# A new order of the query chunks in a differential attention stage

## The chip, the cores and the metric

The kernel runs on one core of one Trainium2 chip. The metric is the device time of one execution in microseconds (us), as the median of three runs. The engines are named as in the profile: PE is TensorE (matmul), PEld its weight load, DVE is VectorE, ACT is ScalarE, POOL is GpSimd, SP is SyncE, which issues the DMAs. Each engine works through its own instructions strictly in the order in which the program lists them; engines wait for one another through semaphores.

## The reference

Two transformer blocks are computed one after the other for 1024 tokens of width 1024. The change touches one stage of the second block, the differential attention of four heads. For each head there are two score maps, their softmaxes are subtracted with a factor, and the difference weighs the values:

```python
def diff_group(dq, dk, dv, q_g, k_g, lq1, lk1, lq2, lk2, out_g, rel_bias, lam_init):
    q = rms_norm(dq.reshape(b, s, DIFF_HEADS, 2, DIFF_QK), q_g)
    k = rms_norm(dk.reshape(b, s, DIFF_HEADS, 2, DIFF_QK), k_g)
    ...
    def one_block(args):
        qb, blk = args                       # 128 query tokens
        allowed = chunk_allowed(q_idx, k_idx)  # 64-token chunks up to the query's own
        bias = table[t5_bucket(k_idx[None, :] - q_idx[:, None])].transpose(2, 0, 1)
        logits = jnp.einsum('bhqmd,bhmkd->bhmqk', qb, k_t).astype(f32) * scale
        logits = logits + bias[None, :, None]
        logits = jnp.where(allowed[None, None, None], logits, NEG_INF)
        probs = jax.nn.softmax(logits, axis=-1)
        attn = (probs[:, :, 0] - lam * probs[:, :, 1]).astype(v_t.dtype)
        return jnp.einsum('bhqk,bhkd->bhqd', attn, v_t)
```

Query chunk t (0 to 7) sees the key tiles 0 to t only. The eight chunks of a head are independent of one another, so they can be computed in any order.

## The kernel before

The program is written out by hand, engine by engine, with one function for each stage and engine. The differential attention is `pe_diff`, `act_diff` and `dve_diff`, with `pe_diff_values`, `act_diff_copies`, `diff_turn` and the preparation of the next head (`pe_diff_prepare`, `act_diff_norms`, `act_diff_parts`, `dve_diff_norms`, `dve_diff_parts`) beside them.

The work is cut into 32 items, one for each head and query chunk. Item n belongs to head n // 8, and `diff_item(n)` says which chunk t it takes. Its size S is t + 1 key tiles of 128 tokens. Before the change the sizes run 1, 2, ..., 8 in heads 0 and 2 and 8, 7, ..., 1 in heads 1 and 3. All engines run the same loop over steps; in step s

- PE first makes four transposes of the next head's queries or keys (L2501), but only in steps 4 to 7 of a head that has a successor. Then it makes the scores of item s (L2638, and the mask L2641). Then it transposes the weights of item s-3 in blocks of up to four tiles (L2651) into PSUM bank 6, and behind each such block it multiplies the block before by the values (L2671). An item of five to eight tiles has two blocks; it is called a two-block item here. For it, the values of its first block stand in its own step, behind its second block's transposes.
- ACT first makes, in steps 4 to 7, the high part of the next head's queries or keys out of bank 6 (L2531). Then come the copy of item s-3's first block (L2694), the exponentials of item s in two passes (L2723), with the copy of a second block between them, and at the end of some steps a square (L2510, L2514) or a root for the next head's norms.
- DVE first makes the low part (L2562) in steps 4 to 7. Then come the weights of item s-2 (L2771, L2773, L2778), the two bias passes of item s (L2790), which read the scores out of PSUM, and the "put" of item s-4 (L2797), which moves the finished output out of bank 7. At the end of some steps it adds a reduction (L2539) or a product (L2548) for the next head: reductions at the end of step 7 and of step 0, products at the end of steps 2 and 3.

The waits that matter are these. The scores of item n+1 wait for the first bias pass of item n. The values of item n's first block wait for the put of item n-1, as both use bank 7:

```python
        if c == 0 and n:
            pe.wait_ge(*self.s("df_put").at(n - 1))
```

The next head's transposes and the turned blocks share bank 6, so each waits until ACT and DVE have read what stands there (`turn_bank_free`). Behind the last item, PE puts the first matmuls of the next stage (L2867 to L2869, `pe_mla_up`) between the rest of the items' blocks.

Of the kernel before, what the change touches and what calls it, by code (L numbers as in the profile page):

```python
# [19 lines left out]
TT = T // P  # L20
# [65 lines left out]
class Kernel:  # L86
# [2341 lines left out]
    def score(self, p, cols, qh, ql, kh, kl):  # L2428
# [4 lines left out]
                mm = self.mm3([self.PS[:, 2 * p + h, 0:n]], qh, ql, [kh[:, c]], [kl[:, c]], True, True)  # L2433
        return mm

    def diff_item(self, n):
        h, t = n // TT, n % TT
        return h, t if h % 2 == 0 else TT - 1 - t

    def groups(self, ap, c=64):  # L2440
        return ap.rearrange("p (g c) -> p g c", c=c)
# [1046 lines left out]
```

## Time and profile before

| | us |
|---|---|
| median of three runs | 2967.72 |
| lowest and highest | 2965.39, 2972.66 |
| the profiled execution | 2988.82 |
| its span, first to last instruction | 2987.5 |
| PE busy in the span | 2875.9 (96%) |
| DVE busy | 1858.2 (62%) |
| ACT busy | 1204.7 (40%) |
| granted TensorE clock, mean over the span | 0.967 |

The profiled execution is 21.1 us longer than the median of the runs. PE is busy nearly all the time, but not everywhere: the second line of the page, which cuts the span into 40 slices, shows 7 and 7 tenths in the slices from 1718 to 1867 us. This is the differential attention. In those slices the granted clock is also below full speed.

### The profile page before, as it was taken

The page shows a single profiled execution, that of the slowest core. Times are in us where ns is not written, and L with a number is a line of the kernel's source. Part 1 is how long each engine was busy: PE and PEld are TensorE (multiplying, and loading weights), DVE is VectorE, ACT ScalarE, POOL GpSimd, SP SyncE. Part 2 cuts the span into 40 slices and gives each one's busy share as a digit, 9 for nine tenths or more (in the row PEclk, how much of TensorE's full clock was granted, in tenths as well). Part 3 has the DMA queues.
Part 4 walks back from the last instruction along what each step waited for, and adds up shares of the span by engine and source line. Part 5 has one row for each costly group of instructions (what it writes and reads, how often), then busy time and mean ns, then how long its engine had stood idle before and what let it go on. Part 6 is the DMA issues. An engine that isn't in the chain of part 4 may idle for free.

```text
span 2987.5 us, 36065 instructions
## 1 busy us (share of the span) xinstructions
PE 2875.9 (96%) x14312; PEld 2407.0 (81%) x14312; DVE 1858.2 (62%) x2615; ACT 1204.7 (40%) x1810; POOL 68.9 (2%) x44
## 2 busy tenths in 40 slices
PE   8999999999999999999999977899999999999998
PEld 6888878887788888888778856788887888888887
DVE  4148766625766666666641277577457777777774
ACT  3144454634433323334331265776433333333432
POOL 0002210010000000000000000000000000000000
PEclk9999997999999999999999988888999999999999
DMA  4111220032211111113121100000211111111122
GB/s 169 50 36 57 79 99 1 6 123 78 106 56 50 51 57 52 50 54 127 50 92 57 37 14 10 22 1 1 92 43 42 50 57 57 47 53 57 56 93 85
DMA packets 47831, 172.99 MB, mean 58 GB/s; under 512 B 5648, under 2 KB 6160, under 8 KB 47664
## 3 DMA queue, kind: packets, MB, share of 16 engines
q1 hardware_dynamic: 47664, 170.68, 17.1%
q8 instruction: 115, 1.88, 0.3%
q14 instruction: 52, 0.43, 0.0%
HBM read 145.23 MB, written 25.43 MB: 57 GB/s over the span
## 4 chain that ended last, share of the span: by engine, by line
PE 87%; DVE 8%; ACT 3%; issue 2%; DMA 0%; SPq 0%; DVEq 0%; ACTq 0%
PE PS L295 14%; PE PS L297 14%; PE PS L299 14%; PE PS L1598 8%; PE PS L1599 8%; PE PS L1600 8%; PE PS L483 2%; PE PS L485 2%; PE PS L484 2%; PE PS L1186 2%; PE PS L706 2%; PE PS L1156 1%; PE PS L1171 1%; PE PS L3118 1%; DVE H L2790 1%
## 5 line engine op out<-in xcount | busy, mean ns | idle before, releaser
L289 DVE TENSOR_TENSOR w_lo<-w_raw,w_hi 128x1024 fp32r<-128x1024 f32 x93 | 117.1, 1262 | 203.1 <-ACT w_hi L283 203.1
L1598 PE MATMUL PS<-u_hi_f,w_hi 128*128 128x512 f32 x624 | 242.7, 389 | 0.0
L1599 PE MATMUL PS<-u_lo_f,w_hi 128*128 128x512 f32 x624 | 242.7, 389 | 0.0
L1600 PE MATMUL PS<-u_hi_f,w_lo 128*128 128x512 f32 x624 | 242.7, 389 | 0.0
L1547 ACT ACTIVATE w_hi<-weight_sums 128x512 fp32r<-128x512 f32 x156 | 98.1, 629 | 356.0 <-DVE weight_sums L1568 197.1
L283 ACT ACTIVATE w_hi<-w_raw 128x1024 fp32r<-128x1024 f32 x93 | 97.6, 1054 | 263.4 <-PE PS L485 136.5
L295 PE MATMUL PS<-f_ah,w_hi 128*128 128x512 f32 x640 | 197.1, 389 | 0.1
L297 PE MATMUL PS<-f_al,w_hi 128*128 128x512 f32 x640 | 197.0, 389 | 0.0
L299 PE MATMUL PS<-f_ah,w_lo 128*128 128x512 f32 x640 | 197.0, 389 | 0.0
L1553 DVE TENSOR_TENSOR w_lo<-w_raw,w_hi 128x512 fp32r<-128x512 f32 x205 | 137.3, 688 | 92.9 <-ACT w_hi L1547 92.9
L1598 PE MATMUL PS<-f_T_hi,w_hi 128*128 128x512 f32 x468 | 182.8, 390 | 1.9 <-issue 1.9
L1600 PE MATMUL PS<-f_T_hi,w_lo 128*128 128x512 f32 x468 | 182.8, 391 | 0.0
L1599 PE MATMUL PS<-f_T_lo,w_hi 128*128 128x512 f32 x468 | 182.6, 390 | 0.0
L1553 DVE TENSOR_TENSOR w_lo<-weight_sums,w_hi 128x512 fp32r<-128x512 f32 x156 | 107.2, 687 | 62.2 <-ACT w_hi L1547 62.2
L295 PEld LDWEIGHTS PS<-f_ah,w_hi 128*128 128x128 f32 x640 | 120.1, 188 | 25.3 <-issue 0.5
L297 PEld LDWEIGHTS PS<-f_al,w_hi 128*128 128x128 f32 x640 | 120.1, 188 | 25.0
L299 PEld LDWEIGHTS PS<-f_ah,w_lo 128*128 128x128 f32 x640 | 120.1, 188 | 24.9
L295 PE MATMUL PS<-u_hi,w_hi 128*128 128x512 f32 x384 | 126.9, 412 | 13.5 <-DVE u_lo L416 13.5
L1598 PEld LDWEIGHTS PS<-u_hi_f,w_hi 128*128 128x128 f32 x624 | 117.1, 188 | 24.4
L1599 PEld LDWEIGHTS PS<-u_lo_f,w_hi 128*128 128x128 f32 x624 | 117.1, 188 | 24.3
L1600 PEld LDWEIGHTS PS<-u_hi_f,w_lo 128*128 128x128 f32 x624 | 117.1, 188 | 24.3
L1660 DVE TENSOR_TENSOR Y<-Y,PS 128x1024 f32<-128x1024 f32 x80 | 97.6, 1220 | 52.3 <-PE PS L299 52.3
(447 smaller groups left out, 6612.4 us busy)
## 6 DMA issues: line engine op xcount, KB each, us to landing
w_raw<-in_weights SPq DMA_DIRECT2D x215, 512.0 KB, 3.6
H<-in_x_t SPq DMA_DIRECT2D x16, 512.0 KB, 4.3
h_kept<-H SPq DMA_DIRECT2D x16, 512.0 KB, 5.1
H<-h_kept SPq DMA_DIRECT2D x16, 512.0 KB, 6.7
stick_kept<-stick_stage SPq DMA_DIRECT2D x12, 512.0 KB, 2.8
mixer<-stick_kept SPq DMA_DIRECT2D x9, 512.0 KB, 6.8
p_kept<-p_stage SPq DMA_DIRECT2D x8, 512.0 KB, 4.0
p_pp<-p_kept SPq DMA_DIRECT2D x8, 512.0 KB, 8.1
```

The source lines that it names most:

```text
L283: act.activation(self.w_hi[i][:], self.w_raw[i][:], ACT.Copy).then_inc(*self.s("w_hi").up(g))
L289: dve.tensor_tensor(self.w_lo[i][:], self.w_raw[i][:], self.w_hi[i][:].bitcast(F32), ALU.subtract).then_inc(*self.s("w_lo").up(g))
L295: ins = e.matmul(banks[i], lh, rh[i], start=first, stop=False)
L297: ins = e.matmul(banks[i], lh, rl[i], start=False, stop=False)
L299: ins = e.matmul(banks[i], ll, rh[i], start=False, stop=last)
L483: pe.matmul(self.PS[:, t, :], UH[:, k, tok], wh, start=first, stop=False)
L1547: act.activation(self.w_hi[room][:, cols], src, ACT.Copy).then_inc(*self.s("w_hi").up("block", n, m))
L1553: dve.tensor_tensor(self.w_lo[room][:, cols], src, self.w_hi[room][:, cols].bitcast(F32), ALU.subtract).then_inc(*self.s("w_lo").up("block ...
L1598: pe.matmul(out, hi[:, self.chunk(k)], rh, start=opens and k == 0, stop=False, skip_group_check=True)
L1599: pe.matmul(out, hi[:, self.chunk(k)], rl, start=False, stop=False, skip_group_check=True)
L1600: mm = pe.matmul(out, lo[:, self.chunk(k)], rh, start=False, stop=k == 3, skip_group_check=True)
L1660: dve.tensor_tensor(Y[:, c, :], Y[:, c, :], self.pair(p), ALU.add).then_inc(*self.dve_frees(p, tag, "down", i, c))
```

## The change

Every head now takes its query chunks in the order 2, 5, 4, 3, 1, 7, 6, 0, so that the sizes run 3, 6, 5, 4, 2, 8, 7, 1 in each head.

```diff
+    DIFF_ORDER = (2, 5, 4, 3, 1, 7, 6, 0)
+
     def diff_item(self, n):
-        h, t = n // TT, n % TT
-        return h, t if h % 2 == 0 else TT - 1 - t
+        return n // TT, self.DIFF_ORDER[n % TT]
```

The number and the shapes of the instructions stay the same. They are listed in another order on PE, ACT and DVE. The line numbers of the stage go up by one.

The first place is step 4 of the second head on PE, from the scores to the transposes that open step 5. In a row, df_kh and df_qh are parts of keys and queries, ident with H is a block being turned, df_at with mixer_196 are the turned weights and the values, and df_staged is the next head. Before:

```order
L2638 MATMUL PS<-df_kh_206,df_qh_204 128x512 x2
L2638 MATMUL PS<-df_kl_207,df_qh_204 128x512 x2
L2638 MATMUL PS<-df_kh_206,df_ql_205 128x512 x2
L2641 MATMUL PS<-df_mask,sb_ident 128x128 x2
L2651 MATMUL PS<-ident,H 128x128 x4
L2671 MATMUL PS<-mixer_196,df_at_212 128x128 x4
L2651 MATMUL PS<-ident,H 128x128 x3
L2671 MATMUL PS<-mixer_196,df_at_211 128x128 x4
L2501 MATMUL PS<-ident,df_staged_219 128x128 x4
```

Now:

```order
L2639 MATMUL PS<-df_kh_206,df_qh_204 128x256 x2
L2639 MATMUL PS<-df_kl_207,df_qh_204 128x256 x2
L2639 MATMUL PS<-df_kh_206,df_ql_205 128x256 x2
L2642 MATMUL PS<-df_mask,sb_ident 128x128 x2
L2652 MATMUL PS<-ident,H 128x128 x4
L2672 MATMUL PS<-mixer_196,df_at_211 128x128 x3
L2652 MATMUL PS<-ident,H 128x128 x2
L2672 MATMUL PS<-mixer_196,df_at_212 128x128 x4
L2502 MATMUL PS<-ident,df_staged_219 128x128 x4
```

The scores in this step shrink from four key tiles to two, and the item being turned from seven tiles (four and three) to six (four and two). Both before and now, four values matmuls and then the next head's transposes stand at the end.

The second place is DVE in step 5 of the second head, from the low part (L2562, now L2563) to the first bias pass (ISA). Before:

```order
L2562 SCALAR_TENSOR_TENSOR df_ql_201<-PS,df_gq,df_qh_200 128x512
L2771 RECIPROCAL df_small<-df_small 128x2
L2773 TENSOR_SCALAR df_small<-df_small,df_nlam 128x1
L2778 SCALAR_TENSOR_TENSOR H<-H,df_small 128x640
L2790 ISA H,df_small<-PS,df_bias_209 128x384
```

Now:

```order
L2563 SCALAR_TENSOR_TENSOR df_ql_201<-PS,df_gq,df_qh_200 128x512
L2772 RECIPROCAL df_small<-df_small 128x2
L2774 TENSOR_SCALAR df_small<-df_small,df_nlam 128x1
L2779 SCALAR_TENSOR_TENSOR H<-H,df_small 128x512
L2791 ISA H,df_small<-PS,df_bias_209 128x1024
```

The bias pass at this place grows from three tiles to eight, and the weights product before it shrinks from five tiles to four.

The third place is the end of the stage on PE, from the last item's mask to the first matmul of the next stage. Before:

```order
L2641 MATMUL PS<-df_mask,sb_ident 128x128 x2
L2651 MATMUL PS<-ident,H 128x128 x4
L2671 MATMUL PS<-mixer_196,df_at_212 128x128
L2651 MATMUL PS<-ident,H 128x128 x3
L2671 MATMUL PS<-mixer_196,df_at_211 128x128 x4
L2867 MATMUL PS<-w_hi_53,mla_lh_223 128x384
```

Now:

```order
L2642 MATMUL PS<-df_mask,sb_ident 128x128 x2
L2652 MATMUL PS<-ident,H 128x128 x2
L2672 MATMUL PS<-mixer_196,df_at_212 128x128 x4
L2652 MATMUL PS<-ident,H 128x128 x4
L2672 MATMUL PS<-mixer_196,df_at_211 128x128 x2
L2652 MATMUL PS<-ident,H 128x128 x4
L2672 MATMUL PS<-mixer_196,df_at_212 128x128 x4
L2868 MATMUL PS<-w_hi_53,mla_lh_223 128x384
```

Before, one block of four and one block of three tiles are turned here, and five values tiles are multiplied. Now a block of two tiles and both blocks of an eight-tile item are turned, and ten values tiles are multiplied. Behind these rows an item of seven tiles is still to be turned, where it was one of two.

## Rows read from the trace of the kernel before

**Rows 1.** The page: busy time of the engines, and the chain by engine.
```profile
PE 2875.9 (96%) x14312; PEld 2407.0 (81%) x14312; DVE 1858.2 (62%) x2615; ACT 1204.7 (40%) x1810; POOL 68.9 (2%) x44
...
PE 87%; DVE 8%; ACT 3%; issue 2%; DMA 0%; SPq 0%; DVEq 0%; ACTq 0%
```

**Rows 2.** Windows: us; busy us of PE, PEld, DVE, ACT, POOL; PEclk; DMA.
```profile
1720.00:1877.00 157.00, 122.70 (x803) 97.21 (x804) 117.40 (x278) 96.75 (x201) 0.00 (x0) 0.86 0.03 8
...
1723.90:1740.80 16.90, 14.29 (x65) 10.49 (x65) 13.40 (x38) 11.22 (x27) 0.00 (x0) 0.50 0.00 0
...
1777.00:1798.00 21.00, 16.79 (x134) 13.82 (x132) 14.37 (x35) 12.29 (x27) 0.00 (x0) 1.00 0.01 1
...
1836.40:1839.70 3.30, 0.96 (x9) 0.80 (x9) 3.23 (x8) 2.27 (x4) 0.00 (x0) 1.00 0.03 8
...
1839.80:1843.10 3.30, 3.30 (x16) 2.05 (x14) 0.57 (x1) 0.17 (x2) 0.00 (x0) 0.50 0.07 25
```

**Rows 3.** Timeline of PE, items 23 to 25 (start, length, engine, line).
```profile
1840.16 0.79 PE L2638 MATMUL PS<-df_kh,df_qh 64*128 64x512 f32 x2
...
1846.45 1.89 PE L2671 MATMUL PS<-mixer,df_at 128*128 128x128 f32 x8 [1.33 <-ACT df_at L2694]
...
1848.28 0.79 PE L2638 MATMUL PS<-df_kh,df_qh 64*128 64x512 f32 x2
```

**Rows 4.** Timeline of DVE, bias passes of items 23 to 25, and a put.
```profile
1837.32 1.22 DVE L2790 CUSTOM_DVE_ANT_0 H<-PS,df_bias 128x1024 f32<-128x1024 f32 x1
...
1843.67 1.23 DVE L2790 CUSTOM_DVE_ANT_0 H<-PS,df_bias 128x1024 f32<-128x1024 f32 x1 [3.29 <-PE PS L2641]
...
1844.82 1.22 DVE L2790 CUSTOM_DVE_ANT_0 H<-PS,df_bias 128x1024 f32<-128x1024 f32 x1
...
1845.96 0.34 DVE L2797 TENSOR_SCALAR mixer<-PS,df_small 128x128 f32<-128x128 f32 x1
...
1851.98 1.09 DVE L2790 CUSTOM_DVE_ANT_0 H<-PS,df_bias 128x896 f32<-128x896 f32 x1
```

**Rows 5.** Timeline of PE, ACT and DVE, items 12 and 13.
```profile
1787.71 1.13 PE L2671 MATMUL PS<-mixer,df_at 128*128 128x128 f32 x8 [1.06 <-DVE mixer L2797]
...
1788.68 0.60 PE L2501 MATMUL PS<-ident,df_staged 128*128 128x128 f32 x4
...
1789.31 0.69 ACT L2531 ACTIVATE df_qh<-PS,df_gq 128x512 fp32r<-128x512 f32 x1 [0.70 <-PE PS L2501]
...
1790.04 0.75 DVE L2562 SCALAR_TENSOR_TENSOR df_ql<-PS,df_gq,df_qh 128x512 fp32r<-128x512 f32 x1 [2.47 <-ACT df_qh L2531]
...
1792.01 0.55 DVE L2790 CUSTOM_DVE_ANT_0 H<-PS,df_bias 128x384 f32<-128x384 f32 x1
```

**Rows 6.** Timeline of ACT and DVE, items 6 to 7.
```profile
1748.49 1.04 ACT L2723 ACTIVATE H<-H,df_small 128x896 f32<-128x896 f32 x1 [0.94 <-DVE df_small L2790]
...
1751.50 0.66 ACT L2531 ACTIVATE df_kh<-PS,gains 128x512 fp32r<-128x512 f32 x1
...
1755.44 1.22 DVE L2790 CUSTOM_DVE_ANT_0 H<-PS,df_bias 128x1024 f32<-128x1024 f32 x1
```

**Rows 7.** Timeline of DVE: item 9's second pass, then a reduction and a product.
```profile
1770.13 1.09 DVE L2790 CUSTOM_DVE_ANT_0 H<-PS,df_bias 128x896 f32<-128x896 f32 x1
...
1804.81 1.21 DVE L2539 TENSOR_REDUCE df_norms<-df_staged 128x16 f32<-128x1024 f32 x1
...
1813.03 1.22 DVE L2548 TENSOR_TENSOR df_staged<-mixer,df_norms 128x1024 f32<-128x1024 f32 x1
```

**Rows 8.** Timeline of PE and DVE, the last item and behind it.
```profile
1879.30 0.42 PE L2867 MATMUL PS<-w_hi,mla_lh 128*128 128x384 f32 x1
...
1877.14 0.29 DVE L2790 CUSTOM_DVE_ANT_0 H<-PS,df_bias 128x128 f32<-128x128 f32 x1
```

**Rows 9.** Timeline of DVE, the first item's two bias passes.
```profile
1724.20 0.28 DVE L2790 CUSTOM_DVE_ANT_0 H<-PS,df_bias 128x128 f32<-128x128 f32 x1
...
1724.41 0.29 DVE L2790 CUSTOM_DVE_ANT_0 H<-PS,df_bias 128x128 f32<-128x128 f32 x1
```

## The prediction

> **What bounds the kernel now.** I read the page first: PE is busy 96% of the span and holds 87% of the chain that ended last, so time is mostly PE's [rows 1]. A change of order removes no PE work, so it can act only where PE waits or runs at a low clock. The windows view shows such a place. From 1720 to 1877 us, PE is busy 122.7 of 157 us, DVE 117.4, ACT 96.8, and the mean granted clock is 0.86 [rows 2]. No engine is full; each waits for another. So I read the timelines of PE, DVE and ACT there, item by item, and looked at what ends each item's wait.
>
> I measure with one mark for each item: the moment when its first bias pass ends and its second one begins. The marks run from 1724.41 (item 0, [rows 9]) to 1877.14 (item 31, [rows 8]), which is 152.7 us. The distance from one mark to the next is an item's period, and four chains set it.
>
> Chain A, through the put. Item 24 has its marks at 1844.82; its second pass ends at 1845.96, then comes the put, then at 1846.45 the values matmuls of a two-block item, at 1848.28 the scores of item 25, and the next mark is at 1851.98 [rows 3, 4]. The row of 1846.45 names ACT's copy as the releaser, but that copy is of the second block, and these are the values of the first; by the program they wait for the put, as the row of 1787.71 says of its own [rows 5]. PE could not begin them earlier, since the put stands behind both bias passes on DVE. PE and DVE thus take turns here instead of overlapping.
>
> Chain B, through the next head. It is the same up to the values (1787.71), then come the next head's transposes (1788.68), ACT's high part (1789.31), DVE's low part (1790.04), and only then the weights and the bias pass (1792.01) [rows 5].
>
> Chain C, through ACT. Both exponentials of item 6 and a square take 1748.49 to 1751.50, then high part, low part, weights, and the mark of item 7 at 1755.44 [rows 6].
>
> Chain D is DVE's own work where it has most.
>
> **The parts and their cost.** Sizes are in key tiles. A bias pass takes 0.21 us for one tile [rows 9] and 1.15 for eight [rows 4], so about 0.075 + 0.134 S. The low part and the weights of five tiles take 1.97 from 1790.04 to 1792.01 [rows 5]; I give 0.67 to the low part and 1.30 to the weights with their two small instructions, and by the slope of the bias pass W(S) = 0.64 + 0.133 S. Values of four tiles take 0.97 at full clock [rows 5] and 1.83 at half [rows 3]; I take 1.05 with what surrounds them. Scores of eight tiles take 3.5 us at half clock from 1840.16 to the bias pass at 1843.67 [rows 3, 4], so near 1.86 at full clock, and I take 0.6 + 0.157 S. A reduction or product of the next head adds 1.13: it is recorded with 1.21 and 1.22, less the overlap with what follows [rows 7].
>
> At full clock chain A costs: second pass of the item before, 0.5 for put and semaphores, 1.05 values, scores, 0.2, first pass. Chain B: second pass, 0.45, 0.97, 0.63 transposes, 0.73 high part, 0.67 low part, W, first pass. The five terms from 0.97 to W are those of 1787.71 to 1792.01, 4.30 us [rows 5]. Chain C checks with item 7: high part, low part, W(6) and a pass of eight are 0.67 + 0.7 + 1.44 + 1.15 = 3.96, and 1751.50 to 1755.44 is 3.94 [rows 6].
>
> Now the sizes of a head with a successor, 3, 6, 5, 4, 2, 8, 7, 1. Two-block items are turned three steps later, so chain A or B holds one step behind each of them.
> Size 3: D, 0.21 + 0.3 put + 1.13 + W(7) 1.57 + 0.48 = 3.7.
> Size 6: A, 0.48 + 0.5 + 1.05 + 1.54 + 0.2 + 0.88 = 4.65.
> Size 5: A, 0.88 + 0.5 + 1.05 + 1.39 + 0.2 + 0.75 = 4.75.
> Size 4: D, 0.75 + 0.3 + 0.38 + 1.14 + W(6) 1.44 + 0.61 = 4.6.
> Size 2: D with low part, 0.61 + 0.3 + 1.14 + 0.7 + W(5) 1.3 + 0.35 = 4.4.
> Size 8: B, 0.35 + 0.45 + 0.97 + 0.63 + 0.73 + 0.67 + W(4) 1.17 + 1.15 = 6.1.
> Size 7: B, 1.15 + 0.45 + 0.97 + 0.63 + 0.73 + 0.67 + W(2) 0.91 + 1.01 = 6.5.
> Size 1: C, 3.1 + 0.67 + 0.7 + W(8) 1.7 + 0.21 = 6.4.
> Together 41.1 us. The third head has no square at its end: 40.2. The last head has no preparation: size 3 takes 2.6, then 4.65 and 4.75, then 3.3 and 3.9 (DVE with one conversion of 1.2 for the next stage), then A twice for sizes 8 and 7, 5.6 and 5.6, then 3.3: together 33.7. In the first head the first pass ends 0.27 later; then scores of six tiles at half clock (the clock there, PEclk 0.50 [rows 2]) and their pass take 3.7, scores of five with theirs 3.5, and the fourth item 0.75 + 0.38 + 1.14 + 1.44 + 0.61 = 4.3 on DVE. That is 11.8, and with 4.4, 6.1, 6.5 and 6.4 it is 35.2. The sum is 35.2 + 41.1 + 40.2 + 33.7 = 150.2, against 152.7 measured: -2.5.
>
> But the measured 152.7 hold time lost to the clock, and 150.2 do not. Items 8 and 9 take 1755.44 to 1770.13 = 14.69 [rows 6, 7] and items 24 and 25 take 1837.32 to 1851.98 = 14.66 [rows 4], where chain A gives 5.95 + 5.6 = 11.5. The 6.3 us beyond are matmuls at half clock. So at full clock the new order is about 4 us longer than the old one: the old order has chain B on sizes 3, 2 and 1 of one head only, the new one has it on 8 and 7 in three.
>
> What the clock will take is the part that no row shows for the new order. PE was busy 0.96 of 3.30 us before 1839.7, and in the next 3.3 us it ran at 1.2 GHz (PEclk 0.50) while fully busy; from 1777 to 1798, busy 16.8 of 21 us, it kept 2.4 GHz [rows 2]. In the new order PE has 26 us of work in the 41 of a head (scores 10, turning 4, values 9, next head 2, masks in them): in the steps of size 5 and 4 about 4 of 9.4, in those of size 7 and 1 about 5.5 of 12.9. Such idle stretches stand right ahead of chains B and A. Matmuls that sit on the chains at full clock are 2.6 + 2.4 for the A steps (heads two to four), 1.6 + 1.6 for the B steps (heads one to three) and 2.9 + 2.75 for the last head's sizes 8 and 7: 15 + 9.6 + 5.7 = 30 us, each doubled at half clock. The bounds are 0 and +30. In the old order there are 16 such steps at 1.6 to 2.9, some 36, and 6.3 were paid, 0.17; the new one idles more ahead of them, and I take 0.37 of 30, which is 11.
>
> The Trainium skill ("TensorE: Matmul & The Clock Gate", section "Loop structure matters more than you think") says that an eviction by DVE does not break PE's warmth as long as the next matmuls follow. By that rule this term would be 0. The trace does not bear it out here: PE had work of the same loop before and after, and still fell to half clock [rows 2].
>
> The tail costs too. Before, from the last mark (1877.14) to the next stage's first matmul (1879.30) are 2.16 us, all on PE [rows 8]. Now PE must turn both blocks of an eight-tile item there and wait for a put: 3.5. Behind it come both blocks of a seven-tile item, 2.9, where two tiles and three values matmuls took 0.8; and 0.4 more behind that. Together 1.35 + 2.1 + 0.4 = +3.9. PE is the busy engine there, so nothing hides it. The bounds are +2.5 (ten more tiles multiplied at 0.25 us, their turning hidden) and +6 (a put missed twice more).
>
> The sum is -2.5 + 11 + 3.9 = +12.4. Against its own time the profiled execution would be 2988.8 + 12.4 = 3001; it lies 21.1 above the median of the runs, so I forecast 2967.7 + 12.4 = 2980.
>
> **The rivals.** Cheap clock: the half-clock stretches fall on turns that hide behind DVE, and the term is 0 to 4. Then the change is -2.5 + 3.9 + 2 = +3, 2971, no measurable difference. For it speaks that items 12 to 15 of the old order ran mostly at full clock through chain B; against it that those had PE busy 0.8 of the time.
> Dear clock: the idle steps keep PE at half clock through most of each head; 22 of the 30 are paid, 2991. The 16.9 us at half clock at the stage's start, with PE busy 14.3 of them [rows 2], speak for it: the clock does not return at once.
> Faster: chains A and B do not hold, because the small items next to the large ones let DVE reach the put early; each item then takes DVE's own load or ACT's. For three heads size 6 takes 3.6 and size 5 4.3 instead of 4.65 and 4.75, size 8 and 7 fall to ACT's 4.9 and 6.0: 3 x (1.5 + 1.7) = 9.6 less. With the cheap clock, -2.5 - 9.6 + 3.9 + 0 = -8, and with the last head's steps as well -12: 2956. It decides at one point, whether values of a two-block item start before both bias passes of that step are over. Against it stands DVE's fixed order, put behind both passes [rows 4].
>
> **How the numbers follow.** Forecast (2975 to 2987) 0.47, cheap clock 0.26, dear clock 0.15, faster 0.12. Within 0.3% of 2967.7 is 2959 to 2977, about what a measurement can tell from no change. Same: the cheap clock and a small part of the forecast, 0.29. Slower: the rest of the forecast and the dear clock, 0.59. Faster 0.12. The range reaches from 2962 to 2994, which takes in the cheap clock and most of the dear one; the forecast's own range is 2975 to 2987.
>
> **What would show it.** In the profile of the changed kernel the marks of 32 items should span about 161 us (150.2 + 11). Sizes 8 and 7 of the first three heads should take over 6 us each, with DVE waiting for the high part; sizes 6 and 5 at least 4.6, with PE waiting for the put. The mean granted clock from first to last mark should be under 0.86. The first matmul of the next stage should come 3 to 4 us behind the last mark. A span of marks under 148 us would prove the chains wrong, a clock at 0.9 or more the clock term.

## The result and the profile after

| | before | after |
|---|---|---|
| median of seven runs, us | 2967.72 | 2986.08 |
| lowest and highest | 2965.39, 2973.10 | 2982.84, 3002.90 |
| ratio to before, 95% interval | | 1.0075 [1.0058, 1.0092] |
| the profiled execution | 2988.82 | 2986.48 |

The new order is slower. The medians lie 18.4 us apart (a ratio of 1.0062; the ratio above also counts two runs after at about 3002 us). Such longer runs exist for the kernel before too (about 2988 us), and the profile shown ahead of the prediction was one of them. So I took a second profile of the unchanged kernel (called "the second profile of before" from here on): 2968.88 us, which is typical.

The page of the changed kernel answers to [rows 1]; the third and fourth rows are the 40 slices.

```profile
PE 2864.7 (96%) x14312; PEld 2397.9 (80%) x14312; DVE 1858.3 (62%) x2615; ACT 1205.4 (40%) x1810; POOL 68.9 (2%) x44
...
PE   8999999999999999999999977899999999999998
...
PEclk9999999999999999999999978887999999999999
...
PE 87%; DVE 8%; ACT 2%; issue 2%; DMA 0%; SPq 0%; DVEq 0%; ACTq 0%
```

The page as a whole tells almost nothing: engine totals and the chain's shares are those of before. The stage has to be cut out with windows. First the changed kernel: a stretch far ahead of the stage, then first to last mark, then a stretch of items 11 and 12 (sizes 4 and 2 of the second head), then items 13 and 14 (sizes 8 and 7). The columns are those of [rows 2].

```profile
450.00:500.00 50.00, 46.85 (x391) 40.80 (x390) 42.76 (x83) 29.95 (x56) 0.00 (x0) 1.00 0.01 2
1709.19:1869.39 160.20, 120.85 (x773) 98.02 (x774) 112.64 (x271) 92.81 (x195) 0.00 (x0) 0.82 0.03 8
1762.00:1770.00 8.00, 4.39 (x28) 3.58 (x27) 7.67 (x17) 4.34 (x11) 0.00 (x0) 0.76 0.01 2
1770.05:1785.11 15.06, 12.41 (x74) 9.94 (x73) 7.77 (x21) 6.72 (x15) 0.00 (x0) 0.79 0.00 1
```

The same windows of the second profile of before:

```profile
450.00:500.00 50.00, 46.86 (x393) 40.66 (x392) 42.77 (x83) 29.58 (x55) 0.00 (x0) 1.00 0.01 2
1708.30:1856.77 148.47, 117.67 (x796) 94.11 (x797) 113.24 (x271) 93.17 (x196) 0.00 (x0) 0.88 0.03 9
```

And of the first profile of before, the one that [rows 1 to 9] come from:

```profile
450.00:500.00 50.00, 47.99 (x260) 42.40 (x260) 29.05 (x64) 19.05 (x33) 0.00 (x0) 0.62 0.00 1
1724.41:1877.14 152.73, 121.92 (x796) 96.61 (x797) 113.17 (x271) 93.17 (x196) 0.00 (x0) 0.86 0.03 9
```

Two things are to be seen. The first profile of before lost its time in two places: another stage, around 450 us, ran at a granted clock of 0.62 instead of 1.00 (its first mark is at 1724.41 instead of 1708.30, 16.1 us later), and the marks of this stage span 152.73 instead of 148.47. And against the typical execution, the new order's marks span 160.20, which is 11.7 us more, with nearly the same DVE and ACT work.

The whole difference of the two typical profiles is 2985.1 - 2967.6 = 17.5 us of span. It is made of 0.9 ahead of the first mark, 11.7 from mark to mark, 3.6 from the last mark to the next stage's first small transposes (12.4 before, 16.0 now) and 1.3 behind them.

How the marks are lost is read from the timelines. In them, L2672 are values, L2639 scores, L2502 the next head's transposes, L2532 and L2563 its high and low part, L2791 bias passes and L2798 puts. PE of the changed kernel, a chain A step (1752.42 to 1753.48), the next one (1757.45, 1758.51), then two chain B steps at lower clock, and the end of the stage:

```profile
1752.42 1.13 PE L2672 MATMUL PS<-mixer,df_at 128*128 128x128 f32 x8 [1.05 <-DVE mixer L2798]
1753.48 0.50 PE L2639 MATMUL PS<-df_kh,df_qh 64*128 64x512 f32 x2
...
1757.45 1.13 PE L2672 MATMUL PS<-mixer,df_at 128*128 128x128 f32 x8 [0.60 <-DVE mixer L2798]
1758.51 0.50 PE L2639 MATMUL PS<-df_kh,df_qh 64*128 64x512 f32 x2
...
1771.54 1.79 PE L2672 MATMUL PS<-mixer,df_at 128*128 128x128 f32 x8
1773.16 0.60 PE L2502 MATMUL PS<-ident,df_staged 128*128 128x128 f32 x4
...
1779.14 1.50 PE L2672 MATMUL PS<-mixer,df_at 128*128 128x128 f32 x8 [1.94 <-ACT df_at L2695]
1780.42 1.06 PE L2502 MATMUL PS<-ident,df_staged 128*128 128x128 f32 x4
...
1871.92 1.13 PE L2672 MATMUL PS<-mixer,df_at 128*128 128x128 f32 x8 [0.35 <-DVE mixer L2798]
1872.81 0.42 PE L2868 MATMUL PS<-w_hi,mla_lh 128*128 128x384 f32 x1
```

ACT of the changed kernel, the high parts of those two chain B steps:

```profile
1773.80 0.69 ACT L2532 ACTIVATE df_qh<-PS,df_gq 128x512 fp32r<-128x512 f32 x1 [1.46 <-PE PS L2502]
...
1781.52 0.69 ACT L2532 ACTIVATE df_kh<-PS,gains 128x512 fp32r<-128x512 f32 x1 [1.37 <-PE PS L2502]
```

DVE of the changed kernel, the two A steps (1755.20 to 1760.18), then the two B steps:

```profile
1755.20 0.96 DVE L2791 CUSTOM_DVE_ANT_0 H<-PS,df_bias 128x768 f32<-128x768 f32 x1 [1.03 <-PE PS L2642]
...
1756.96 0.34 DVE L2798 TENSOR_SCALAR mixer<-PS,df_small 128x128 f32<-128x128 f32 x1
...
1760.18 0.82 DVE L2791 CUSTOM_DVE_ANT_0 H<-PS,df_bias 128x640 f32<-128x640 f32 x1 [1.84 <-PE PS L2642]
...
1770.05 0.42 DVE L2791 CUSTOM_DVE_ANT_0 H<-PS,df_bias 128x256 f32<-128x256 f32 x1
...
1771.04 0.35 DVE L2798 TENSOR_SCALAR mixer<-PS,df_small 128x128 f32<-128x128 f32 x1 [0.56 <-PE PS L2672]
1774.52 0.75 DVE L2563 SCALAR_TENSOR_TENSOR df_ql<-PS,df_gq,df_qh 128x512 fp32r<-128x512 f32 x1 [3.13 <-ACT df_qh L2532]
...
1776.36 1.22 DVE L2791 CUSTOM_DVE_ANT_0 H<-PS,df_bias 128x1024 f32<-128x1024 f32 x1
...
1777.50 1.22 DVE L2791 CUSTOM_DVE_ANT_0 H<-PS,df_bias 128x1024 f32<-128x1024 f32 x1
...
1778.64 0.35 DVE L2798 TENSOR_SCALAR mixer<-PS,df_small 128x128 f32<-128x128 f32 x1
1782.24 0.75 DVE L2563 SCALAR_TENSOR_TENSOR df_kl<-PS,gains,df_kh 128x512 fp32r<-128x512 f32 x1 [3.25 <-ACT df_kh L2532]
```

Read the A step: the put at 1756.96, the values at 1757.45, the scores at 1758.51, the bias pass at 1760.18, and DVE waited 1.84 us for the scores. Nothing overlaps: PE stood still before the values, DVE behind its weights product. Read the first B step (size 8): the mark at 1770.05, the put at 1771.04, values 1771.54, transposes 1773.16, high part 1773.80, low part 1774.52, first pass 1776.36, next mark 1777.50. That is 0.99 + 0.50 + 1.62 + 0.64 + 0.72 + 1.84 + 1.14 = 7.45. The prediction gave 6.1 for it; the 1.3 more are in the first and third term, where the put waits for values of the item before (0.56) and these values take 1.62 instead of 0.97. Both are matmuls at the lower clock.

The row at 1779.14 names ACT's copy as what ended the wait, as the row of 1846.45 did [rows 3]; by the program these values wait for the put, which began at 1778.64. Where the put alone was moved, the wait at this place shrank from 1.94 to 0.79 us (below).

Periods by size, with those predicted; the ones with preparation are of the second head. The 5.6 predicted for size 8 of the last head is a slip: the terms of chain A behind size 2 give 0.35 + 0.5 + 1.05 + 1.86 + 0.2 + 1.15 = 5.11, which is what was measured.

| size | 3 | 6 | 5 | 4 | 2 | 8 | 7 | 1 |
|---|---|---|---|---|---|---|---|---|
| predicted, full clock | 3.7 | 4.65 | 4.75 | 4.6 | 4.4 | 6.1 | 6.5 | 6.4 |
| second head | 4.16 | 4.63 | 4.85 | 4.57 | 4.55 | 7.45 | 7.61 | 6.41 |
| last head, predicted | 2.6 | 4.65 | 4.75 | 3.3 | 3.9 | 5.6 | 5.6 | 3.3 |
| last head | 2.79 | 6.29 | 4.84 | 3.06 | 3.71 | 5.11 | 5.60 | 3.19 |

### The profile page after: what moved, and what is told of

The parts are those of the page before. It is cut to its first block, busy times and chain, and to the rows that moved or that the text cites. A ratio compares the mean times of both kernels' runs of the same rounds, so it can differ in the third digit from the quotient of the medians.

```text
span 2985.1 us, 36065 instructions
## 1 busy us (share of the span) xinstructions
PE 2864.7 (96%) x14312; PEld 2397.9 (80%) x14312; DVE 1858.3 (62%) x2615; ACT 1205.4 (40%) x1810; POOL 68.9 (2%) x44
## 4 chain that ended last, share of the span: by engine, by line
PE 87%; DVE 8%; ACT 2%; issue 2%; DMA 0%; SPq 0%; DVEq 0%; ACTq 0%
PE PS L295 14%; PE PS L297 14%; PE PS L299 14%; PE PS L1598 8%; PE PS L1599 8%; PE PS L1600 8%; PE PS L485 2%; PE PS L483 2%; PE PS L484 2%; PE PS L1186 2%; PE PS L706 2%; PE PS L3119 1%; PE PS L1156 1%; PE PS L1171 1%; PE PS L2672 1%
```

## The experiments

The unchanged kernel and eleven variants ran in three groups, each on another chip; the kernel before ran with each group, at medians of 2969.02, 2967.34 and 2967.62, so the groups can be compared to within about 2 us. Ratios are to before. "New" and "old" are the two orders. Marks are read from one profile of each kernel. Where I write that an item is at half clock, the mean granted clock over its period is below 1.00 and the period is longer than that of the same step at 1.00 elsewhere.

**The unchanged kernel again.**

> The kernel before once more, to have a profile of a usual execution. The theory (all of the change's cost is made in the differential attention and in the stage's tail) expects marks of the 32 items to span 152 to 153 us as in the first profile, and the stick-breaking stage near 450 to 500 us, which stood at PEclk 0.62 in the first profile of before and at 1.00 in that of the changed kernel, to be at full clock; total 2968. The rival (the first profile was not typical in the differential attention either) expects marks to span some 147 us, 5 to 6 us less, since that much of the measured 18 us is not explained by the two first profiles.

Measured: 2967.99, ratio 0.9989 [0.9962, 1.0015]. Its profile is the second one above, with marks of 148.47: nearer to the rival's 147 than to the theory's 152. The stretch at 0.62 around 450 us and 4.3 us of this stage belong to the execution, not to the order.

**The put moved forward.** The put of item s-4 stands between the two bias passes of item s instead of behind both. Nothing is added or left out.

```diff
                                              small[:, s, m:m + 1]).then_inc(*self.s("df_biased").up(n, m))
-            n = step - 4
-            if 0 <= n < N:
...
+                    if m == 0:
+                        self.dve_diff_put(step - 4)
+            else:
+                self.dve_diff_put(step - 4)
```

In the new order:

> The new order, with the put of item n-4 between the two bias passes of item n instead of behind them. If the put behind two passes sets the steps behind two-block items, these start their values up to one pass earlier: about 1.1 us less at size 7 behind size 8 and 0.3 at size 5 behind size 6, some 1.4 us for each of four heads, so marks span about 155 us instead of 160.2 and the total is 4 to 5 us less. The rival (idle and clock set these steps, not the put) expects no change within 1 us, or 1 to 2 us more, as the second pass comes later.

Measured: 2975.64, ratio 1.0011 [0.9986, 1.0037], 10.4 us under the new order. Marks span 151.69 instead of 160.20. I had expected 4 to 5 us. Size 7 of the second head takes 5.95 instead of 7.61, size 5 4.02 instead of 4.85. Size 2 and size 1 grew, to 5.71 and 7.37 from 4.55 and 6.41, since DVE now waits for values before its second pass. The second head's sizes 8 and 7 in a window, and the put between the passes of size 2 and of size 1:

```profile
1769.18:1780.93 11.75, 9.92 (x74) 7.57 (x73) 7.59 (x20) 6.15 (x13) 0.00 (x0) 1.00 0.00 1
...
1768.91 0.35 DVE L2755 TENSOR_SCALAR mixer<-PS,df_small 128x128 f32<-128x128 f32 x1 [0.91 <-PE PS L2672]
...
1788.03 0.35 DVE L2755 TENSOR_SCALAR mixer<-PS,df_small 128x128 f32<-128x128 f32 x1 [0.64 <-PE PS L2672]
```

Not all of the 8.5 us of marks is the chain through the put: the same window ran at 0.79 before this edit and runs at 1.00 now. Steps at 1.00 in both profiles show the put alone: size 5 falls by 0.83 and the last head's size 7 by 1.09. The six B steps fall by 8.2 us, but with the added matmuls below, and the put where it was, four of them take 6.15 and 6.54, against 5.80 and 5.95 here. So most of their fall is clock that came back. With every half-clock loss taken off both profiles, 151.4 us of marks become 150.0: some 1.4 of the 8.5 us are the put's, because sizes 2 and 1 take back most of what the other steps gain.

In the old order:

> The old order with the put between the bias passes. put_mid_new won 0.8 to 1.1 us at each large item behind a two-block item but lost 1.0 to 1.15 at sizes 2 and 1 of the preparation steps, where DVE now waits for the values before its second pass. The old order has 8 to 12 steps of the first kind (about 8 us won in all) and 12 preparation steps (up to 1 us lost in each), so the theory of the put chain expects between 6 us less and 4 us more, about -1; the rival, that put_mid_new won by a luckier clock, expects 5 us or more less here too, with the gain in steps that no put stands before.

Measured: 2958.87, ratio 0.9953 [0.9928, 0.9977]. That is 8.5 us faster than the kernel before, and the fastest of all that ran with the whole work in it. I had expected between 6 less and 4 more, about 1 less; the falling heads gain more than the rising ones lose. Marks span 140.32 instead of 148.47. About 3 of these 8.15 us are clock: items 8 and 17, at 0.64 and 0.50 in the second profile of before, are at 0.88 and 1.00 here. The last head shows the put alone, from the mark of item 23 to that of item 31, in the second profile of before and then here, 3.5 us less with the clock at 1.00 in both:

```profile
1820.02:1856.77 36.75, 30.96 (x241) 25.43 (x242) 29.11 (x68) 24.05 (x50) 0.00 (x0) 1.00 0.02 5
...
1814.76:1847.98 33.22, 31.16 (x243) 25.78 (x243) 29.20 (x69) 24.77 (x52) 0.00 (x0) 1.00 0.02 5
```

DVE of this kernel, item 25:

```profile
1822.86 1.09 DVE L2797 CUSTOM_DVE_ANT_0 H<-PS,df_bias 128x896 f32<-128x896 f32 x1 [0.28 <-PE PS L2641]
...
1823.87 0.35 DVE L2754 TENSOR_SCALAR mixer<-PS,df_small 128x128 f32<-128x128 f32 x1
1824.14 1.08 DVE L2797 CUSTOM_DVE_ANT_0 H<-PS,df_bias 128x896 f32<-128x896 f32 x1
```

And its PE there:

```profile
1824.37 1.13 PE L2671 MATMUL PS<-mixer,df_at 128*128 128x128 f32 x8
```

The values begin 0.5 us behind the put, beside the second pass; DVE waited 0.28 us for the scores. In the kernel before, the values come behind that pass [rows 3, 4]. The period of this item falls from 5.61 to 4.49.

**The last head taken from 8 down to 1**, the rest in the new order.

```diff
-        return n // TT, self.DIFF_ORDER[n % TT]
+        return n // TT, TT - 1 - n % TT if n // TT == DIFF_H - 1 else self.DIFF_ORDER[n % TT]
```

> The new order in three heads, sizes 8 to 1 in the last. By the four chains the last head takes 33.9 us instead of 34.6 and the tail is 3.7 us shorter (a two-tile item is left instead of a seven-tile one), so the total is 4 to 5 us less than with the new order, about 14 us over before. The rival, that most of the loss comes from the end of the stage and from what it does to the next one, expects it to be 10 us less or more.

Measured: 2978.17, ratio 1.0031 [1.0006, 1.0057], 8 us under the new order, between the 4 to 5 that I expected and the rival's 10. Marks span 160.05, so the last head itself gains nothing, and the way from the last mark to the next stage's small transposes is 12.4 us again instead of 16.0. The tail term of 3.6 is shown; every profile whose order ends in 7, 1 has 15.7 to 16.0 there, and every one that ends in 2, 1 has 11.6 to 12.4. For the other 4 us of the median the profile is no guide: it is of the shortest of ten runs (2973.22), with its first mark 5.6 us earlier than in the new order and 3.8 us less behind the small transposes, neither of which this edit touches. I leave them open.

**No preparation of the next head.** The kernel leaves out the next head's transposes, high and low parts and norms. The diff shows PE; the same lists are emptied on ACT and DVE, and PE no longer waits for the next head's low part.

```diff
-        side = self.sides([self.pe_diff_prepare(h) for h in range(1, DIFF_H)], TT)
+        side = self.sides([], TT)
...
-                qh, ql, kh, kl = self.df_sets[h % 2]
+                qh, ql, kh, kl = self.df_sets[0]
...
```

In the new order:

> The new order without any preparation of heads 1 to 3: their normalised queries and keys are left out, and all heads use those of head 0. By the chains every head then costs what the last one costs less its conversions for the next stage, about 32 us, so marks span about 130 us, 30 us less. Theory: what the new order loses is lost where the next head's preparation meets large items, so without it the new order is within 4 us of the old order without it (run in the next call). Rival: the new order loses by its clock and by the put alone, and stays 12 us or more behind.

Measured: 2951.83, ratio 0.9930 [0.9907, 0.9953]. Marks span 128.04.

In the old order:

> The old order without any preparation of heads 1 to 3 (all heads use the queries and keys of head 0), to stand beside no_next_new (2951.8 us, marks 128.0). If the new order loses by the meeting of preparation and large items, the old order without preparation is no more than 4 us faster than 2951.8, or even slower, since it has 8 behind 8 twice: marks 124 to 132 us, total 2946 to 2952 (the tail alone is 3.7 shorter). If the loss comes from put and clock alone, it is 12 us or more faster: below 2940.

Measured: 2937.25, ratio 0.9881 [0.9848, 0.9914]. Marks span 118.30. This is where my theory fell. I held that the new order loses because the preparation meets its large items. Without any preparation it is still 14.6 us behind, 9.7 of it between the marks; preparation costs 30.2 us of marks in the old order and 32.2 in the new one. So only about 2 of the 11.7 us hang on it. Half clock does not hang on it either: three items of the new order without preparation (7.27, 7.17 and 7.17, where the same steps otherwise take 5.11, 5.60 and 5.60) hold 5.3 of the 9.7. The rest, 4.4, is there at full clock.

DVE of the old order without preparation, three items of a rising head:

```profile
1770.61 0.56 DVE L2788 CUSTOM_DVE_ANT_0 H<-PS,df_bias 128x384 f32<-128x384 f32 x1
...
1772.74 0.68 DVE L2788 CUSTOM_DVE_ANT_0 H<-PS,df_bias 128x512 f32<-128x512 f32 x1
...
1775.26 0.82 DVE L2788 CUSTOM_DVE_ANT_0 H<-PS,df_bias 128x640 f32<-128x640 f32 x1
```

DVE of the new order without preparation, sizes 6 and 5:

```profile
1775.05 0.96 DVE L2789 CUSTOM_DVE_ANT_0 H<-PS,df_bias 128x768 f32<-128x768 f32 x1 [2.16 <-PE PS L2640]
...
1780.01 0.82 DVE L2789 CUSTOM_DVE_ANT_0 H<-PS,df_bias 128x640 f32<-128x640 f32 x1 [1.82 <-PE PS L2640]
```

The first three rows name no wait: DVE works without a gap, and PE's scores are hidden. In the other two DVE waits about 2 us each time. This led to the count that I had not made (a "turn" here is a step in which PE and DVE wait for one another). Item k is taken in turns (chain A or B) when item k-4 has two blocks. In the old order these are the eight items of every falling head, sizes 8 to 1, 36 tiles, and none of a rising head. In the new order they are sizes 8, 7, 6 and 5 of every head: also eight in two heads, but 52 tiles. In such a step the scores are exposed and the weights product of item k-2 is hidden; elsewhere it is the other way round. So two heads of the new order expose 16 more tiles of scores at 0.157 = 2.5 us, and hide the weights of 20 tiles instead of 48, 28 at 0.133 = 3.7 us: 6.2 by this count. Without preparation two heads take 58.0 in the old order (the third, rising, 21.2, and the last, falling, 36.8), and 2 x 31.46 = 62.9 in the new one (its second head twice), all at full clock: 4.9. The count fits in sign and size, but no run tests its two terms apart. Twice 4.9 would be 9.8 over all four heads, and only 4.4 shows. The first heads, which both begin at half clock, make the gap: from its second item on, the old order's is 4.1 us longer than its third head, while the new order's, with no turns yet on sizes 6 and 5, is 1.8 shorter than its second (its size 8, counted above, taken at 5.11).

**Three heads rising, the last falling.**

```diff
-        return h, t if h % 2 == 0 else TT - 1 - t
+        return h, t if h < DIFF_H - 1 else TT - 1 - t
```

> The old order with the second head turned round: sizes 1 to 8 in heads 0, 1 and 2 and 8 to 1 in the last. By the chains the two-block items of a rising head are turned beside the small items of the next head, where values and put are short, and no preparation step stands behind a two-block item but the last. Head 1 should take 38.5 us from mark to mark instead of 45 to 49, so marks span 144 us instead of 148.5 and the total is 3 to 6 us under the kernel before. The rival (the order of sizes matters only by what it does to the clock) expects the kernel before's time within 2 us.

Measured: 2967.87, ratio 0.9991 [0.9967, 1.0014]: no difference where I expected a gain of 3 to 6 us. A miss; the rival's number came true. Marks span 149.62, in a profile of the longest run (2985.26, clock 0.62 around 450 us), so they are compared with care. The count tells where the expectation went wrong: behind a rising head, items of sizes 1 to 4 stand four behind two-block items, and here that is so in two heads. The second head does fall, from 46.34 us to 40.65. But the third, which stood behind a falling head and now stands behind a rising one, goes from 34.35 to 39.73: its sizes 1 and 2 take 4.57 and 5.53 instead of 2.71 and 3.95. The one pays for the other.

**All heads falling.** By the count its turns fall on sizes 4, 3, 2 and 1 of every head. The first item's scores also wait for the second half of the keys, which a size 8 needs.

```diff
-        return h, t if h % 2 == 0 else TT - 1 - t
+        return n // TT, TT - 1 - n % TT
```

> Sizes 8 to 1 in every head (the first scores wait for the second half of the keys as well). New theory after no_next_old (the new order stays 14.6 us behind without any preparation): the number of steps behind two-block items is the same in both orders, but such a step costs about 0.29 us for each key tile of its own item, since scores and first pass stand on the chain, while the weights product of the item two before it is hidden. The new order puts these steps on sizes 6, 5, 8, 7, the old one on 8 to 1 of every second head, this one on 4, 3, 2, 1 of each. It expects marks of 149 to 153 us and a total of 2968 to 2973, 13 to 18 us under the new order. The rival, that rising heads are what makes the old order fast, expects 2980 or more, as with two such heads lost.

Measured: 2971.71, ratio 1.0020 [1.0007, 1.0033]; marks span 150.21 (again in a profile of the longest run). It also uses one order for every head, also has eight steps of turns in two heads, and is 14 us faster than the new order, as the count expected. It is not the sameness of the heads that costs. That the sizes on which the turns fall make the rest, beside the last sizes, is what the count says; this run agrees with it.

**More matmuls ahead of three scores of the new order.** They write where the scores then write.

```diff
+                if n % TT in (3, 4, 7) and h < DIFF_H - 1:
+                    for i in range(3):
+                        for m in range(2):
+                            rows = slice(64 * m, 64 * m + 64)
+                            pe.matmul(out[m][:, 0:HALF], qh[rows, self.chunk(t)], kh[rows, 0:HALF], start=True,
+                                      stop=True, skip_group_check=True)
```

> The new order with six further matmuls of 512 columns (64 rows each) ahead of the scores of sizes 4, 2 and 1 in the first three heads, where PE idles; they write a bank that the scores then overwrite. The result is the same. If half clock on chain B costs 1.1 us at each size 8 and each size 7 of three heads, as the profile of the new order reads (7.3 to 7.6 instead of 6.1 and 6.5), then PE at full clock there gives back 4 to 7 us, with these periods under 6.8. If the chain itself is longer than I reckoned and the clock does not matter, the time stays or rises by up to 3 us.

Measured: 2979.37, ratio 1.0038 [1.0018, 1.0058]. PE has 54 more matmuls and the kernel is 6.7 us faster than the new order. Marks span 153.62 instead of 160.20. The windows of this kernel that answer to 1762 to 1770 and to items 13 and 14 above:

```profile
1763.00:1771.00 8.00, 5.41 (x44) 4.19 (x41) 7.67 (x18) 4.68 (x11) 0.00 (x0) 1.00 0.00 0
1770.98:1783.67 12.69, 9.54 (x72) 7.56 (x73) 7.60 (x19) 6.47 (x14) 0.00 (x0) 1.00 0.01 2
```

Its PE at the first of the B steps:

```profile
1771.82 1.13 PE L2678 MATMUL PS<-mixer,df_at 128*128 128x128 f32 x8 [0.50 <-DVE mixer L2804]
1772.79 0.60 PE L2502 MATMUL PS<-ident,df_staged 128*128 128x128 f32 x4
```

The values take 0.97 again, the clock is 1.00, and sizes 8 and 7 of the second head take 6.15 and 6.54, as against 6.1 and 6.5 predicted at full clock; the third head takes the same. In the first head it worked in part only: 6.43 and 7.54, the latter at a clock of 0.77. The six B steps together fall by 5.8 us, which is the clock's part that this run shows. Size 6 of the last head falls by 1.6, though no matmuls were added in that head, and other steps grow by 0.9.

**The put forward only where it helps**, in steps that follow turns. With `mid` false the put stands behind both passes.

```diff
+            mid = 3 <= step < N and self.diff_item(step - 3)[1] >= 4
...
+                    if m == 0 and mid:
+                        self.dve_diff_put(step - 4)
+            if n >= N or not mid:
+                self.dve_diff_put(step - 4)
```

In the old order:

> The old order, the put between the bias passes only in steps whose turned item has two blocks, else behind them as before. It should keep the gain of put_mid_old (8.5 us) and not lose the 0.2 to 0.3 us at each of sizes 5 to 8 in the preparation steps of the rising heads: marks 138 to 140 us, total 2956 to 2959, the fastest so far. The rival: moving the put back there wins nothing, 2959.

Measured: 2961.01, ratio 0.9980 [0.9959, 1.0001]. I had expected 2956 to 2959: a miss by 2 us. The rising heads went back to their old periods but for size 8, and item 8 took 7.21 us in this profile at a clock of 0.62 and item 17 3.74. It is not better than moving all puts.

In the new order:

> The new order with the same rule. Against put_mid_new (2975.6) it should win back the 1.0 us at size 1 of three heads, where the put now stands behind both passes again: marks 148 to 150 us, total about 2973. The order itself should stay 14 to 18 us slower than put_some_old, since the put's place does not change on which sizes the chain falls. The rival (orders differ only through the put's place) expects them within 5 us.

Measured: 2972.13, ratio 1.0020 [1.0011, 1.0029], and marks of 149.89, both as expected. It stays 11.1 us behind the same edit in the old order, less than the 14 to 18 that I expected and more than the rival's 5.

With three heads rising:

> Sizes 1 to 8 in three heads, 8 to 1 in the last, and the put between the passes behind two-block items. three_up did not win the 3 to 6 us that I expected: sizes 1 and 2 behind size 8 took 4.6 to 5.5 us each instead of 3.7 to 4.4. If that is the put behind size 8's two passes, it now falls by about 1 us at each of some four such steps for each rising head, as in the old order, and the total is 2954 to 2959. If it is PE's own work on size 8 (turning and values at half clock), the gain is under 5 us: 2963 or more.

Measured: 2960.68, ratio 0.9968 [0.9949, 0.9988]. It is 7.2 under the kernel without the edit, which lies between the two answers that I had named and decides nothing.

Not tried: a second place in bank 7 for the values, which would free them of the put. It would let PE write and DVE read the same bank with no order between them.

## Why the prediction was right, and where not

The forecast was 2980.0 with a range of 2962 to 2994, slower at 0.59; measured were 2986.1, slower. Step by step:

**The chains.** Right. Sizes 6 and 5 took 4.63 and 4.85 (said: 4.65 and 4.75), with PE waiting for the put, and sizes 8 and 7 took 6.15 and 6.54 once the clock was full (said: 6.1 and 6.5). Moving the put shortened steps that ran at full clock before and after: 0.83 at size 5, 3.5 us over the old order's last head. The rival "faster", with values ahead of both bias passes, has no step in the trace; it came about only where the program was changed to allow it.

**The marks.** Said were about 161 us, measured 160.2. That it came so close is luck in part: the clock term was 2.2 too high and the rest 1.2 too low (below), although that rest holds a slip of +0.5 at size 8 of the last head.

**The clock term.** Right in kind. Said was a mean clock under 0.86, measured 0.82 [rows 2 for before]. The added matmuls gave 5.8 back at the six B steps. The share of 0.37 that made 11 out of 30 was a guess between the bounds of 0 and 30; no row gave it, and 8.8 of 30 would be 0.29. Counted by periods, the six B steps on sizes 8 and 7 lie 1.1 to 1.4 over 6.15 and 6.54 and the last head's size 6 1.65 over 4.64: 8.8 in all. So 11 was somewhat too much, and the rest of the marks, 151.4, somewhat more than the 150.2 that I had worked out.

The Trainium skill's rule ("TensorE: Matmul & The Clock Gate", section "Loop structure matters more than you think"), that an eviction by DVE does not break the warmth, is given for matmuls that follow immediately. I took it to make the term 0, which was a misreading: here PE waits for DVE or ACT before most of these steps (1.57 and 1.94 us at items 12 and 14), so this case does not put that rule to the test. The same page of the Trainium skill, section "A second HAM failure mode: psum-queue depth-cycling", describes a loop whose short idle times between groups of matmuls make the clock go up and down; the trace agrees with that in kind (clock 0.76 with PE busy 4.39 of 8.00 us, 1.00 with the added matmuls).

**The tail.** Said +3.9, measured +3.6; the first matmul of the next stage 3.4 us behind the last mark (said: 3 to 4).

**The step that failed: "the sum is -2.5 + 11 + 3.9 = +12.4", laid on the median.** The first two terms were taken against the first profile's 152.7 us of marks, and the whole 21.1 us between that execution and the median were treated as lying elsewhere. The second profile shows that 16.1 of them did, and 4.3 were half-clock steps of this very stage. Against the typical 148.5 the same working gives 161.2 - 148.5 + 3.9 = +16.6, or 2984. Measured were +18.4.

**A reason that failed: "the old order has chain B on sizes 3, 2 and 1 of one head only, the new one has it on 8 and 7 in three".** Taken as the cause it fell: without preparation, and so without any chain B, 9.7 of the 11.7 us remain. By periods, the typical old order loses 3.1 us to half clock (items 8 and 17), the new one 8.8; so 5.7 of the 11.7 are clock and 6.0 are there beside it, of which 4.4 remain without preparation. By the count they come from the sizes that the turns fall on at all, 52 tiles of scores in two heads against 36, through chain A as much as chain B. The periods in the prediction contained this, since each was worked out by its own chain, so the sum did not suffer; the sentence that explained it did.

Shown by runs: that the put's place sets the turns, 5.8 us of the clock's part, the tail, and that preparation is not the cause. Only argued: that the 6.0 us beside the clock come from the sizes in the turns (the runs with all heads falling and three heads rising agree with the count, none isolates it), the split of the 4.9 us in two heads into scores and weights, and why the new order loses more to the clock (it has more such turns on large items, with PE idle ahead of them). Open: 4 us of the run with the last head falling, and how much of each gain by the put is clock that came back with it. The clock parts are counted from one profile of each kernel.

## What to carry to other kernels

Before work of different sizes is reordered, mark the steps in which engines take turns instead of overlapping, and count which sizes the new order puts there and which stands last; here the order with large items in them was slower though the work is the same. Look first at what releases the turn: moving one short instruction between two long ones gained 8.5 us, some 3 of them through the clock, and none of the other orders tried gained anything. Where such an edit also changes the clock, compare steps that run at the same clock in both profiles. And take two profiles of a kernel before a sum is laid on its median, since one execution can hold a stretch at half clock just where the change acts.

## What the runs showed of the hardware that was not expected

Profiles of the same program can differ in one stage, around 450 us, that the change does not touch: the window from 450 to 500 us has a granted clock of 0.62 in three of the fourteen profiles (the first of before, three heads rising, all heads falling) and 0.97 to 1.00 in the others, and in those three the first mark comes at 1724 to 1726 us instead of 1703 to 1711. Why it comes is open.

PE got faster by more work: 54 matmuls of 512 columns more, and 6.7 us less. They lie in steps where PE otherwise waits for DVE, so they cost little on the path, and in five of the six B steps behind them the clock was 1.00, where it had been 0.78 to 0.82.

The clock fell without any long wait of PE: in the new order without preparation, the size 7 of the third head took 7.17 us at a clock of 0.76, where the same step took 5.60 at 1.00 in the second head. From 1784 us to the half-clock values at 1793.08 us the waits of PE were 1.13, 0.55, 0.24 and 1.35 us.
